# When GpSimd issues the small loads of the next attention block: after the ninth down product instead of after the last set's seventh product

## The reference

```
for l in range(DEPTH):
    x = x + 0.5 * swiglu(rmsnorm(x, ffn1_norm[l]), ffn1_wg[l], ffn1_wu[l], ffn1_wd[l])
    h = rmsnorm(x, mix_norm[l]) @ w_in[l]
    h_a, h_b, h_c = jnp.split(h, [A_COLS, A_COLS + B_COLS], axis=-1)
    o_a = mla_mixer(h_a, cs_a, mla_q_norm[l], mla_kv_norm[l], mla_w_uq[l], mla_w_ukv[l])
    o_b = nsa_mixer(h_b, cs_b, nsa_pe_k[l], nsa_pe_v[l], nsa_phi_k1[l], ...)
    o_c = diff_mixer(h_c, cs_c, diff_lq1[l], diff_lk1[l], ..., diff_sub_norm[l], l)
    x = x + jnp.concatenate([o_a, o_b, o_c], axis=-1) @ w_out[l]
    x = x + 0.5 * swiglu(rmsnorm(x, ffn2_norm[l]), ffn2_wg[l], ffn2_wu[l], ffn2_wd[l])
return rmsnorm(x, final_norm)
```

## Time and profile before

| | |
|---|---|
| time, median of 3 runs | 1558.7 us (1558.41 to 1558.72) |
| time of the profiled execution | 1558.86 us |
| its span | 1557.0 us |
| TensorE busy | 1531.7 us, 98% of the span |
| VectorE busy | 1310.7 us, 84% |
| ScalarE busy | 1021.7 us, 66% |
| GpSimd busy | 155.3 us, 10% |
| mean DMA rate | 206 GB/s |

### The profile page before, as it was taken

One profiled execution on the slowest core, in us unless ns is written; L12 is line 12 of the kernel. 1 busy time (PEld: TensorE's weight loads), 2 busy tenths in 40 slices (PEclk: granted clock), 3 DMA queues, 4 the chain that ended last, 5 costly groups with the idle time before them and its releaser, 6 DMA issues.

```text
span 1557.0 us, 21001 instructions
## 1 busy us (share of the span) xinstructions
PE 1531.7 (98%) x8060; PEld 1262.1 (81%) x8060; DVE 1310.7 (84%) x1420; ACT 1021.7 (66%) x1400; POOL 155.3 (10%) x232
## 2 busy tenths in 40 slices
PE   9999999999999999999999999999999999999998
PEld 7778888877888888888777788888888887788886
DVE  6869998786999989997658699988999766789996
ACT  7756776675677657665657567665667556657674
POOL 1001000040100010002021000000000203000000
PEclk9999999999999999999999999999999999999999
DMA  8338888623888867899540387977798752067983
GB/s 302 128 110 252 233 267 242 197 80 118 299 228 239 263 207 239 258 284 249 169 150 2 119 260 220 280 231 250 238 282 230 245 188 82 1 233 239 291 230 115
DMA packets 154611, 321.17 MB, mean 206 GB/s; under 512 B 5736, under 2 KB 50016, under 8 KB 151440
## 3 DMA queue, kind: packets, MB, share of 16 engines
q1 hardware_dynamic: 135408, 261.87, 48.0%
q0 software_dynamic: 18672, 57.42, 18.9%
q10 hardware_dynamic: 432, 0.53, 0.1%
HBM read 293.59 MB, written 1.05 MB: 189 GB/s over the span
## 4 chain that ended last, share of the span: by engine, by line
PE 92%; DVE 4%; ACT 2%; DMA 1%; issue 1%; POOL 0%; SPq 0%; POOLq 0%; DVEq 0%; ACTq 0%
PE pair L2893 10%; PE pair L2894 10%; PE pair L2897 10%; PE pair L2804 8%; PE bank L2774 6%; PE bank L2978 6%; PE bank L2970 6%; PE bank L2974 6%; PE pair L2808 4%; PE bank L2747 3%; PE bank L2680 2%; PE bank L2681 2%; PE bank L2682 2%; PE pair L3184 2%; PE bank L3235 1%; PE pair L2953 1%
## 5 line engine op out<-in xcount | busy, mean ns | idle before, releaser
L1688 DVE TENSOR_TENSOR w_lo<-raw,w_hi 128x2048 fp32r<-128x2048 f32 (+2 forms) x167 | 378.3, 2272 | 43.8 <-ACT w_hi L1052 43.4
L1052 ACT ACTIVATE w_hi<-raw 128x2048 fp32r<-128x2048 f32 (+2 forms) x171 | 324.7, 1902 | 50.3 <-DMA raw<-in_w_in 10.1
L1688 DVE TENSOR_TENSOR w_lo<-fold_raw,w_hi 128x2048 fp32r<-128x2048 f32 x144 | 327.3, 2287 | 19.5 <-ACT w_hi L1052 19.2
L1052 ACT ACTIVATE w_hi<-fold_raw 128x2048 fp32r<-128x2048 f32 x144 | 275.7, 1915 | 75.1 <-PE bank L2978 38.3
L2894 PE MATMUL pair<-w_hi,xs_lo 128*128 128x512 f32 x384 | 149.9, 390 | 0.0
L2893 PE MATMUL pair<-w_hi,xs_hi 128*128 128x512 f32 x384 | 149.7, 390 | 0.0
L2804 PE MATMUL pair<-xt,w_hi 128*128 128x512 f32 x528 | 129.0, 394 | 0.1
L2893 PE MATMUL pair<-w_hi,xt 128*128 128x512 f32 x288 | 113.8, 395 | 0.0
L2804 PEld LDWEIGHTS pair<-xt,w_hi 128*128 128x128 f32 x528 | 97.3, 188 | 19.5 <-issue 0.5
L2894 PE MATMUL pair<-w_hi,xt 128*128 128x512 f32 x288 | 112.3, 390 | 0.0
L2970 PE MATMUL bank<-w_hi,hid_hi 128*128 128x512 f32 x424 | 106.3, 390 | 0.0
(11 more groups left out here) (362 smaller groups left out, 2859.0 us busy)
## 6 DMA issues: line engine op xcount, KB each, us to landing
raw<-in_ffn_wd SPq DMA_DIRECT2D x44, 1024.0 KB, 9.4
fold_raw<-in_w_gate_up SPq DMA_DIRECT2D x32, 1024.0 KB, 7.0
fold_raw<-in_ffn_wu SPq DMA_DIRECT2D x32, 1024.0 KB, 6.8
fold_raw<-in_ffn_wg SPq DMA_DIRECT2D x32, 1024.0 KB, 6.7
fold_raw<-fold_raw POOLq DMA_DIRECT2D x24, 1024.0 KB, 7.7
raw<-in_w_down SPq DMA_DIRECT2D x22, 1024.0 KB, 9.1
raw<-in_w_in SPq DMA_DIRECT2D x21, 1024.0 KB, 6.5
fold_raw<-in_ffn_wu POOLq DMA_DIRECT2D x16, 1024.0 KB, 11.6
```

What stands on the lines that cost most here:

```text
L1052: act.activation(w_hi[u % RING][:, 0:filled(u)], raw_of(u)[:, 0:filled(u)], ACT.Copy)\
L1688: dve.tensor_tensor(w_lo[s][:, 0:filled(u)], raw_of(u)[:, 0:filled(u)], w_hi[s][:, 0:filled(u)].bitcast(F32), ALU.subtract)\
```

## The change

GpSimd's wait ahead of the sixteen DMAs asks for a higher count of unit_used. FOLD_AT[3][5] is place 39, DOWN_AT[8] is place 42. Both passes are changed, since the line stands in the loop over the layers. No instruction is added, removed or moved on any engine; the number in one wait differs, twice.

```
                 fold_sums(2 + 2 * l)
-                pool.wait_ge(unit_used, ffns[2 + 2 * l][0] + FOLD_AT[FOLDS - 1][5] + 1)
+                pool.wait_ge(unit_used, ffns[2 + 2 * l][0] + DOWN_AT[8] + 1)
                 for dst, src in (
                     (uq[:, 0:576], a["mla_w_uq_2"][l, 0:P, :]),
                     (uq[0:HD, 576:1152], a["mla_w_uq_2"][l, P:A_QR, :]),
```

## The result

The changed kernel takes 1561.92 us (median of 19 runs, 1560.68 to 1563.62) against 1558.86 us of before in the same series (19 runs, 1556.99 to 1559.81): a ratio of 1.0019, with a 95% interval of 1.0012 to 1.0025. It is 3.1 us slower. The forecast was 0.8 us faster, and 1561.92 lies inside its range of 1554.0 to 1562.5, close to the upper end; the direction was wrong.

The account below looks back on a forecast made before the run. The prediction took TensorE as the bound, busy nearly throughout. First pass -5.0 + 2.1 and second pass + 2.1 made -0.8 us: 1557.9 us against a median of 1558.7, range 1554.0 to 1562.5.

Parts of the forecast that it names:

- I take 7.2 us: W2's time from issue to landing beside the small loads, 2.2 us late against 5.0.
- 2.1 us in each pass: TensorE's idle before the transposes: W2 2.2 us late, less 0.1 of slack, in both passes.
- W2 over 8 us: Stated sign that the prediction is wrong: W2 landing in under 6 us or over 8.
- I take it as staying: TensorE's granted clock keeps the upper level behind the new waits; if it falls, 1.7 us more in that pass.
- the 5.0 of the sum: First pass, up to the projection: 5.0 us regained from the stall behind W1, 3.34 of lateness plus 1.67 of clock.
- the main case with the lower clock behind one or both waits: Rival, chance 0.12: -0.8 plus 1.7 or 3.4 us, a time of 1559.6 to 1561.3.
- the main case: Chance 0.50: W2 takes 6.5 to 8.2 us, idles 1.4 to 3.1, clock unchanged; 1556.5 to 1559.9 us.
- blocked as W1 was: Rival, chance 0.15: W2 takes 9.4 us in both passes, +7.0, 1565.7 us; in one pass only, 1561.8.
- a W2 of 7.6 us in each pass with the clock held: The point where the two idles and their clock together exceed the 5.0 us gained, turning the change slower.
- The change does not free W1: Rival, chance 0.08: the first pass's 5.0 us not regained in full; with a third regained +2.5, 1561.2 us.
- W2 isn't hurt: Rival, chance 0.15: W2 lands within 0.5 us of now, only the gain is left, 1553.7 to 1554.7 us.
- At worst twice: By the skill's turn-taking rule, W2 sharing the queues would at worst take twice its unshared time, 10 us.

Follow-up runs that it names:

- run 1: Against the kernel before: all of GpSimd's small loads wait for W2's landing, in both passes; 1554.79 us, ratio 0.9973.
- run 8: Against the changed kernel: all sixteen small loads wait one down product longer, for the tenth; 1555.08 us, ratio 0.9976 against the kernel before.
- run 9: The changed kernel with W2 read from other memory (ffn1_wd_2), in rows of 1024 floats instead of 512; 1558.53 us, ratio 1.0001 against the kernel before.
- run 6: Against the changed kernel: only the seven spread loads start at the ninth down product; uq, ukv and phi wait for W2's landing; 1564.18 us.
- run 5: Against the changed kernel: only big (uq twice, ukv) starts at the ninth down product; spread and phi loads wait for W2's landing; 1559.87 us.
- run 2: Against the kernel before: the change in the second pass alone, the first keeping the wait for the seventh product; 1562.23 us, ratio 1.0022.
- run 7: Against the kernel before: big and phi loads keep the seventh-product wait, the seven spread loads wait for W2's landing; 1554.91 us, ratio 0.9975.
- run 3: Against the kernel before: the small loads wait for the last set's sixth product, 5.4 us earlier; 1557.38 us, ratio 0.9989.
- run 4: Against the changed kernel: the six phi loads wait for W2's landing, the other ten start with the ninth down product; 1561.63 us, ratio 1.0018.

## Why the prediction was wrong

**The path was right, two terms on it were not.** The small loads start at 733.4 behind L2978; W1 lands in 5.2 us and nothing waits for it; W2 becomes the last thing waited for, in both passes; the chain from its landing to the transposes has no slack. Runs 1 and 8 take the small loads away from both W1 and W2, and gain 3.9 us each. The users of the small loads wait for no DMA: VectorE's lamv row stands behind other work:

```profile
761.11 0.18 DVE L2448 CUSTOM_DVE_ANT_0 junk<-lamv 128x32 f32<-128x32 f32 x1
```

**The term that was mis-sized is "I take 7.2 us" for W2.** It measured 8.5 and 8.1. With 5.0 taken off, 3.5 and 3.1 us late instead of 2.2. Against "2.1 us in each pass" the stretch from the down product to the transposes is longer by 745.85 - 732.01 - 10.44 = 3.40 us in the first and by 3.04 in the second: 2.2 us more than forecast for both. The prediction's own sign of being wrong, W2 over 8 us, came true in both passes. The estimate leaned on a twin, the last ffn_wd load, which took 6.5 us from the same position. The prediction named the difference that broke the twin, rows of 512 floats against 1024, and put too little on it. Run 9 comes closest to measuring it: with long rows, from other memory, a W2 beside the same loads takes 6.9. The prediction also held that W2 would be nearly through when the slow stretch of the small loads came. Run 6 shows that the spread loads delay W2 even when they start with it. What they do in the changed kernel's own order, behind big, is not told: leaving them out (run 5) saves 1.3 and 0.5 us, no more than the scatter of landings.

**The clock, "I take it as staying", failed in the first pass.** The granted clock was 0.58 behind 3.24 us of idle, which cost the 1.7 us that the prediction had priced. The corrections give the result: -0.8 + 2.2 + 1.7 = +3.1 us. This is the account of one profiled execution of each kernel. That it meets the difference of the medians to 0.1 us is partly luck, because on both sides the clock falls in some executions and not in others. The kernel before loses 5.0 us by its stall in its profile and 3.3 in run 2's, and runs 1, 7 and 8, which remove the stall, gain 3.9 to 4.0 in the median. So the 5.0 of the sum was probably about 1 us too high for the median, though run 1's interval does not rule it out.

**The rivals.** The nearest was "the main case with the lower clock behind one or both waits" (0.12), with 1559.6 to 1561.3: the clock fell behind one. Of W2's landings 8.1 is just inside the main case (6.5 to 8.2) and 8.5 outside, both below "blocked as W1 was" (9.4) and both beyond the point from which the sign was to turn, "a W2 of 7.6 us in each pass with the clock held". That point may have been a little too high: run 9, with 6.9 twice, took 0.4 us less than before, and run 5, with 7.2 and 7.6 and the clock held in its profile, 0.9 more, though neither is told from no change. The chance for slower, 0.23, was too small: the bounds 6.5 and 9.4 lay on both sides of 7.6 and no row favoured the lower half but the twin. "The change does not free W1" is out, by 5.2 us in both passes. "W2 isn't hurt" is out too.

**The Trainium skill's turn-taking** (page "DMA: Bandwidth & Descriptors", section "Queues, rings and completion order") was said to disagree with W1's blocked stretch. For W2 the runs agree with it in kind: a load in short rows loses more beside the same traffic than one in long rows. Two steps of that paragraph do not hold. "At worst twice" needs turns of equal length, and the section doesn't say that: by it a turn is a whole packet, of 9 to 17 descriptors as a rule. And of the 3.6 us in which q1 had a share of 3.6%, the first microsecond is the ordinary start of a load: in the changed kernel, with nothing beside it, q1 moved nothing between 1219.75, where W1 is issued, and 1220.75. Whether the rest, and the 4 us of run 7, are long turns or something else no run here shows; what in big and phi holds W1 for 9.4 to 9.9 us was not taken apart further.

**A correction to the text ahead.** It says that uq lies in the memory of the sets' lower halves. It doesn't: in the second stack those halves take 8192 bytes from the start of that region, and uq begins 9216 bytes behind its start. The seventh product is therefore no bound for the loads, which is why run 3 could place them earlier. No term of the sum used it.

## What to carry to other kernels

A group of background loads doesn't have one cost; its cost is that of the foreground load in flight beside it, so before moving it, list the transfers that TensorE is waiting behind, one after the other, with their slack: here the gap between W2's landing and the need for W3 held them nearly free of charge (runs 1 and 8), and one down product earlier the same loads cost 7 us more. To price a load beside others, use a twin with the same row length as well as the same position. When the point where the sign turns lies between the two bounds, give the other sign more than a fifth.

## What the runs showed of the hardware that was not expected

Rows spread over all partitions cost far more than their bytes: 256 KB of them delayed a 1 MB load by 3.2 and 4.1 us (8.2 and 9.1 against 5.0; run 6), 816 KB in rows of 2.3 and 3.1 KB by 2.2 and 2.6 (run 5).

Whether TensorE's clock falls behind a wait isn't settled by the wait's length alone. It fell behind 2.38 us (run 4, first pass) and 2.75 us (run 2, second pass), and it stayed behind 2.89 (changed kernel, second pass) and 3.02 (run 2, first pass). The granted clock of run 4 behind the 2.38, and of run 2 behind the 3.02 and the 2.75:

```profile
744.00:748.00 4.00, 4.00 (x15) 3.42 (x16) 2.90 (x6) 1.67 (x4) 1.68 (x5) 0.57 1.07 343
```

```profile
746.70:750.70 4.00, 3.93 (x21) 3.37 (x22) 3.60 (x8) 1.57 (x4) 0.00 (x0) 1.00 0.62 234
1238.70:1242.70 4.00, 3.92 (x16) 3.25 (x17) 3.17 (x8) 1.57 (x4) 0.00 (x0) 0.63 0.98 279
```

Each fall costs some 1.7 us, (1 - 0.57) times the 4 us of the stretch in the earlier trace rows. A kernel with waits between 2.38 and 3.02 us may so differ by that much from one execution to the next. The mean granted clock on record for each execution bears this out, though it is given to three places only and includes the kernel's last microseconds. In run 4 the executions at 0.999, 0.998 and 0.997 took 1560.7, 1561.9 and 1563.4 us on average. In the changed kernel the four at 0.999 took 1560.9 and the other fifteen 1562.1. Of the kernel before, in the series of run 1, twelve at 0.999 took 1558.3 and eighteen at 0.998 took 1559.4.
